# Slab splits and norms of a two-block transformer kernel placed anew, and GpSimd's attention slabs subtracted in eight pieces

## The reference

```python
def ffn_half(h, m, k, g_norm, wi, wo):
    hn = modulate(rmsnorm_2(h, g_norm), m[3 * k], m[3 * k + 1])
    return h + 0.5 * m[3 * k + 2][:, None, :] * swiglu(hn, wi, wo)
...
    hn = modulate(rmsnorm_2(h, norm_g[l, 1]), ml[3], ml[4])      # x * (1 + scale) + shift
    qa, ka, va, qb, kb, vb, uc, gl = project_tokens(hn, w_in[l], qk_g[l], cos, sin)
    ...
    h = h + ml[5][:, None, :] * merge_branches(ya, yb, yc, gl, w_branch[l], w_out[l])
```

## Time and profile before

| what | value |
|---|---|
| median of three runs | 3198.99 us (3192.22 to 3200.24) |
| the profiled execution | 3192.69 us, its span 3190.9 us |
| TensorE busy | 2930.7 us (92%) |
| VectorE, ScalarE, GpSimd busy | 1550.4, 1028.4 and 309.9 us |
| mean granted clock of TensorE | 0.964 |
| the second block | from about 1127 us to the end |

### The profile page before, as it was taken

How to read it: one execution, slowest core, us unless ns; L and a number is a source line. 1 busy time by engine, 2 the same in 40 slices (tenths; PEclk the granted TensorE clock), 3 DMA queues, 4 the chain that set the end, 5 groups by cost and what they waited for, 6 DMA issues and landing times.

```text
span 3190.9 us, 55191 instructions
## 1 busy us (share of the span) xinstructions
PE 2930.7 (92%) x23861; PEld 2389.9 (75%) x23861; DVE 1550.4 (49%) x2194; ACT 1028.4 (32%) x1502; POOL 309.9 (10%) x226
## 2 busy tenths in 40 slices
PE   6998877899999889899899989999899998989899
PEld 6876565677767679877568878888688887769899
DVE  6534244233223356673764434444544457476566
ACT  3211113222222244432642332222422224264543
POOL 5123000000000000122100010000100003210000
PEclk9999888999999989999999999999899999999999
DMA  6346857999889845411012222222122222104552
GB/s 243 132 166 260 328 233 314 419 385 373 353 354 383 353 163 185 146 66 40 1 40 106 106 100 98 92 92 93 66 98 100 92 93 80 53 14 176 200 188 85
DMA packets 77069, 547.83 MB, mean 172 GB/s; under 512 B 8384, under 2 KB 10432, under 8 KB 11056
## 3 DMA queue, kind: packets, MB, share of 16 engines
q1 hardware_dynamic: 76000, 540.05, 43.7%
q0 software_dynamic: 848, 4.53, 0.4%
HBM read 637.87 MB, written 1.05 MB: 200 GB/s over the span
## 4 chain that ended last, share of the span: by engine, by line
PE 79%; DVE 10%; DMA 3%; ACT 3%; issue 3%; POOL 1%; DVEq 0%; POOLq 0%; SPq 0%; ACTq 0%
PE bank L759 56%; PE bank L1117 9%; DMA ring<-slabs 3%; PE bank L1467 2%; DVE clow L2536 1%; ACT whi L1913 1%; PE bank L822 1%; DVE tiny L2691 1%; PE bank L952 1%; PE bank L1555 1%; PE bank L939 1%; DVE wk L2668 1%; PE bank L1536 1%; PE bank L1636 1%; PE bank L1644 1%
## 5 line engine op out<-in xcount | busy, mean ns | idle before, releaser
L759 PE MATMUL bank<-hhi,whi 128*128 128x256 f32 (+1 forms) x1280 | 437.3, 342 | 18.7 <-DVE wlo L2145 18.7
L759 PE MATMUL bank<-hlo,whi 128*128 128x256 f32 (+1 forms) x1280 | 435.8, 340 | 0.0
L759 PE MATMUL bank<-hhi,wlo 128*128 128x256 f32 (+1 forms) x1280 | 432.5, 338 | 0.0
L2145 DVE TENSOR_TENSOR wlo<-ring,whi 128x2048 fp32r<-128x2048 f32 x132 | 298.7, 2288 | 266.0 <-ACT whi L1668 208.1
L759 PE MATMUL bank<-fhl,whi 128*128 128x256 f32 (+1 forms) x1408 | 348.0, 339 | 0.0
L1668 ACT ACTIVATE whi<-ring 128x2048 fp32r<-128x2048 f32 x132 | 251.2, 1908 | 211.1 <-PE bank L759 211.1
L759 PEld LDWEIGHTS bank<-hhi,whi 128*128 128x128 f32 x1280 | 242.6, 190 | 48.4 <-issue 19.8
L1117 PE MATMUL bank<-ring,wk 128*32 128x256 f32 x4064 | 252.8, 392 | 22.0 <-DMA ring<-slabs 13.8
L759 PEld LDWEIGHTS bank<-hhi,wlo 128*128 128x128 f32 x1280 | 245.6, 192 | 29.2
L759 PEld LDWEIGHTS bank<-fhl,whi 128*128 128x128 f32 x1408 | 240.3, 188 | 32.0
L759 PEld LDWEIGHTS bank<-hlo,whi 128*128 128x128 f32 x1280 | 243.0, 190 | 28.1
(11 more groups left out here) (492 smaller groups left out, 5562.6 us busy)
## 6 DMA issues: line engine op xcount, KB each, us to landing
ring<-slabs SPq DMA_DIRECT2D x542, 1024.0 KB
wk<-slabs SPq DMA_DIRECT2D x45, 1024.0 KB, 11.5
ac<-slabs SPq DMA_DIRECT2D x16, 1024.0 KB, 10.5
wk<-mixp POOLq DMA_DIRECT2D x1, 1040.0 KB, 12.5
xt<-xT SPq DMA_DIRECT2D x1, 1024.0 KB, 6.7
xt<-ctxT POOLq DMA_DIRECT2D x1, 1024.0 KB, 6.0
out<-xt SPq DMA_DIRECT2D x4, 256.0 KB, 2.4
cst<-maskc POOLq DMA_DIRECT2D x1, 960.0 KB, 14.7
```

The lines of the kernel that those rows point to most:

```text
L759: last = pe.matmul(o, a, b, start=k == 0, stop=k == len(pairs) - 1)
L2145: tt_(wlo_of(n), slab(n), whi_of(rel).bitcast(F32), ALU.subtract).then_inc(sem("wlo"), 1)
```

## The change

It does five things. (1) In block 0 of an FFN ScalarE splits the gate slab of block 1 before the SiLUs, the up slab of block 1 between the SiLUs and the high halves, and the down slab after those; VectorE splits that up slab before the low halves. (2) In the norms in front of FFNs, VectorE applies the scale together with the root, ScalarE adds the shift as it rounds the high half, and VectorE's subtract adds the shift again; the scales of norm n + 1 are computed at the end of norm n. (3) In norm 4 GpSimd adds only tiles 1 and 2 to tile 0, and TensorE sums six tiles. (4) VectorE's two splits for FFN 3 come before tile 3 of the last but one down product and before tile 2 of the last. (5) GpSimd subtracts an attention slab in eight instructions of 256 columns.

```diff
+def added(n):
+    return 2 + 5 * (n - 4) if n >= 4 else 0
...
             def add_squares(n, T):
-                for j in range(1, 6):
+                for j in range(1, 3 if n == 4 else 6):
...
-                    pool.tensor_tensor(wlo_of(n), slab(n), att_whi(l, i).bitcast(F32), ALU.subtract
-                                       ).then_inc(sem("al"), 1)
+                    for q in range(0, SLAB, FB):
+                        c = slice(q, q + FB)
+                        ins = pool.tensor_tensor(wlo_of(n)[:, c], slab(n)[:, c], att_whi(l, i)[:, c].bitcast(F32),
+                                                 ALU.subtract)
+                    ins.then_inc(sem("al"), 1)
...
             def root_rows(n, T):
-                for j in (0, 6, 7):
+                tiles = (3, 4, 0, 5, 6, 7) if n == 4 else (0, 6, 7)
+                for j in tiles:
...
                 if n >= 3:
                     l, k = (n - 3) // 3, (n - 3) % 3
+                    if ph is not None:
+                        for j in range(KT):
+                            act.wait_ge(sem("hs"), 8 * (n - 3) + j + 1)
+                            for half in range(T // TX):
+                                c = slice(half * TX, (half + 1) * TX)
+                                ins = act.activation(high[j][:, c], HT[:, j, c], ACT.Identity,
+                                                     bias=MOD[:, l, 24 * k + j, half:half + 1])
+                            ins.then_inc(sem("hh"), 1)
+                        return
...
                 def step(b, i):
+                    if b == 0:
+                        split_slab(ph, gate_slab(1))
+                        silu(0, 0, None)
+                        silu(0, 1, None)
+                        split_slab(ph, gate_slab(1) + 1)
+                        high(0, 0, None)
+                        high(0, 1, None)
+                        split_slab(ph, down_slab(ph, 0))
+                        return
...
+            def scales(n):
+                l, k = divmod(n - 3, 3)
+                then(ts_(AMOD, MOD[:, l, 24 * k + 8:24 * k + 16, :], 1.0, None, ALU.add))
+                w = pc("ng", 24 * l + 8 * k, 8).rearrange("p (a b) -> p a b", b=1)
+                then(tt_(AMOD, AMOD, w.to_broadcast([P, 8, 2]), ALU.mult))
...
-                        if j < KT:
+                        if j < KT and ph is None:
                             tt_(HT[:, j, 0:T], XT[:, j, 0:T], root, ALU.mult).then_inc(sem("hs"), 1)
-                        if high is not None and j >= 2:
-                            dve.wait_ge(sem("hh"), h0 + j - 1)
+                        elif j < KT:
+                            for half in range(T // TX):
+                                c = slice(half * TX, (half + 1) * TX)
+                                ins = stt(HT[:, j, c], XT[:, j, c], AMOD[:, j, half:half + 1], root[:, c], ALU.mult,
+                                          ALU.mult)
+                            ins.then_inc(sem("hs"), 1)
...
+                        for half in range(T // TX):
+                            c = slice(half * TX, (half + 1) * TX)
+                            ins = stt(HLO[:, j - 2, c], HT[:, j - 2, c], MOD[:, l, 24 * k + j - 2, half:half + 1],
+                                      high[j - 2][:, c].bitcast(F32), ALU.add, ALU.subtract)
+                        ins.then_inc(sem("hl"), 1)
+                    if n < 8:
+                        scales(n + 1)
...
                 def down(b, i):
                     for m in range(nd):
-                        if after is not None and b == ph["nb"] - 1 and m in (0, 4):
-                            split_slab(after, m // 4)
+                        if after is not None and (b, m) in ((ph["nb"] - 2, 3), (ph["nb"] - 1, 2)):
+                            split_slab(after, b - ph["nb"] + 2)
...
                     product(b, 0, i)
                     product(b, 1, i)
+                    if b == 0:
+                        split_slab(ph, gate_slab(1) + 1)
                     low(b, 0, i)
                     low(b, 1, i)
                     if b or i is not None:
                         down(b - 1, i)
+                    if b and not last:
+                        split_slab(ph, gate_slab(b + 1) + 1, i)
                     if not last:
-                        split_slab(ph, gate_slab(b + 1) + 1, i)
                         split_slab(ph, down_slab(ph, b), i)
```

More of the change, by code:

```diff
@@ L778, in root_rows @@
                     else:
-                        pe.wait_ge(sem("sacc"), count("sacc", 5 * (n - 3)))
+                        pe.wait_ge(sem("sacc"), count("sacc", added(n)))
                     for c in range(rows):
                         mm = pe.matmul(bank[3][0:rows, 0:RCOL], pc("erow", 7 - c, rows), HT[:, j, c * RCOL:(c + 1) * RCOL],
-                                       start=j == c == 0, stop=j == 7 and c == rows - 1)
+                                       start=j == tiles[0] and c == 0, stop=j == 7 and c == rows - 1)
                         if owed[0]:
@@ L2145, in split_slab @@
                 tt_(wlo_of(n), slab(n), whi_of(rel).bitcast(F32), ALU.subtract).then_inc(sem("wlo"), 1)
[L2147 to L2154 removed]
+            def scales(n):
[3 more added lines that the diff above has]
+                then(tt_(AMOD, AMOD, w.to_broadcast([P, 8, 2]), ALU.mult))
+            def norm(n, T, ph=None, h0=None, high=None):
+                l, k = divmod(n - 3, 3)
                 if n == 3:
+                    scales(3)
                     split_slab(ph, 0)
```

14 lines of the change are left out of this document (7 added, 7 removed).

## The result

The changed kernel takes 3148.6 us (median of 4 runs, 3144.7 to 3149.9) against 3199.6 us for the kernel before beside it (3192.2 to 3205.2): ratio 0.984, 95% interval 0.982 to 0.986. Its profiled execution has a span of 3142.9 us at a mean granted clock of 0.969, against 3190.9 at 0.964. The forecast was 3151.

The account below looks back on a forecast made before the run. TensorE, busy 92% of the span, bounds the kernel; gains are its idle or lower-clock time. Terms sum to 44.3 us: 3148.4 from the profiled execution, 3154.7 from the median, middle 3151 us; range 3137 to 3170.

Parts of the forecast that it names:

- Stalls (18.7): Behind the first block of each FFN: four waits for VectorE's low half of a slab go, 18.7 us.
- Clock behind them (7.0): Behind the four first-block stalls: without the idle time TensorE's clock does not fall, 7.0 us (bounds 0 and 8).
- the clock does not come back: Rival, chance 0.20: first-block stalls go but the lower clock stays for some microseconds; 7.8 us missing, 3159 us.
- Fused norm: Norms ahead of the four FFNs: high half ready sooner, 1.3 us each for n=5, 6 and 0.8 for n=3, 8; 4.2 us.
- the low end: Fast end of the range, 3137 us: more gain from clock, first blocks, jobs and cheap pieces, 55 us off 3192.
- Norm 4 (2.9): Norm 4: GpSimd adds two tiles, TensorE sums six in 5.7 us, ending at 1339.6 and not 1342.5; 2.9 us.
- Norm 6 (2.0): Ahead of the third FFN, VectorE's splits move earlier: adds end 1.2 us sooner, half the clock's fall 0.8; 2.0 us.
- Norm 7's scale (1.4): Norm 7: a small VectorE scale instruction, lengthened by GpSimd's subtract, is moved away; 1.4 us.
- the projection (1.6): Projection of layer 1: rotations held less by GpSimd's pieces, 5.3 us, against two later slabs; net 1.6 us.
- The term of the slab: GpSimd's attention slab in eight instructions: 6.2 us against 4.6 in one, 1.6 us more.
- Jobs (6.5): Attention jobs: VectorE's scalings wait at most one GpSimd piece, so TensorE idles less; about 6.5 us.
- The likeliest case: Whole kernel: the forecast itself, all terms gained, 3151 us; chance 0.60.

Follow-up runs that it names:

- the early split alone: Kernel before with only the split of gate slab 1 moved ahead of block 0's SiLUs and products: 3184.7 us, ratio 0.995; repeated, 3185.2 us, 0.996.
- filling the idle time alone: Kernel before, its four stalls kept but filled with repeated TensorE products into an unused bank: 3191.7 us, ratio 0.997.
- the pieces alone: Kernel before with only GpSimd's 22 attention slabs subtracted in eight instructions of 256 columns: 3185.7 us, ratio 0.996.
- the norms alone: Kernel before with only the fused norm ahead of the four FFNs and the scale instructions moved to the norm before: 3192.0 us, ratio 0.998.

## Why the forecast was right, point by point

Us gained, by the first traces of both kernels. The table's stretches count each stall with the clock that it met.

```
                                    forecast   measured
1, 2  splits in block 0, clock        25.7       27.3     first blocks 19.5, clock behind them 7.8
3     fused norm of the FFNs           4.2        6.1     2.0 + 1.6 + 1.6 + 0.9, of it 3.6 clock
4     norm 4                           2.9        3.9     3.0 to the end of the root rows, 0.9 behind
5     norm 6                           2.0        2.7
6, 7  norm 7, projections              3.0        1.5     4.1 - 2.4 - 0.2
7     jobs                             6.5        8.5     2.7 + 5.8
      rest of FFN 3 and 4                        -0.4
sum                                   44.3       49.5     (48.0 in span: norm 3 began 1.5 us later)
```

- **Stalls (18.7).** Right. The idle time before L759 went from 18.7 to 0.6 us, and the early split alone cut the net time by 17.6. The up slab of block 1, with its margin of 0.7 us, is not late.
- **Clock behind them (7.0).** Right in place, size and cause: 15.6 us of lower clock behind the four first blocks, worth 7.8, are none after, and filling the idle time alone gave 9.1. The rival "the clock does not come back" falls in all eight traces with the early split: none has any lower clock there. The forecast gave it 0.20; its argument, that the idle time ahead of each first block remains, was true but it only costs within the first block (8.0 us there after, 12.0 before).
- **Fused norm.** From VectorE's first instruction to TensorE's first matmul of FFN 2 it is 2.0 us now (1861.52 to 1863.48) and was 3.5: 1.5 for the 1.3 that I had. The rest of the surplus is clock, which the shorter idle times met less of; I had left that for the low end.
- **Norm 4 (2.9).** Right to 0.1 us up to the end of the root rows. I had TensorE sum six tiles in 5.7 us, and it took 5.53, and starts the moment it comes free.
- **Norm 6 (2.0).** The adds end 1.2 us sooner, as I had it (a wait of 1.87 for 3.11); of the clock's fall I took half, 0.8, and the whole came back, 1.6 (2.85 for 4.47).
- **Norm 7's scale (1.4) and the projection (1.6).** The term of the scale was right: from the end of the root rows of n=7 to TensorE's next matmul it was 2.44 us and is 0.97. But 0.6 us come back right behind it, where the clock costs 1.0 more than before. The projection term was too large: the projections of layer 1 are 3.2 us shorter, the last slabs take 2.4 back and layer 0 0.2, so 0.6 for 1.6. The scale took 3.96 us because GpSimd's slab held it; with pieces, that cause is gone as well, so moving it adds nothing to the pieces. The sum of the forecast has the gain once, and rightly so. In the kernel with the pieces alone, where the scale stands at its old place, its two instructions take 0.17 and 0.65 us:

```profile
2650.08 0.17 DVE L2155 TENSOR_SCALAR tiny<-mods 128x16 f32<-128x16 f32 x1
2650.29 0.65 DVE L2157 TENSOR_TENSOR tiny<-tiny,par 128x16 f32<-128x16 f32 x1
```

  Norm 7 with its projections is 4.7 us shorter by the pieces alone, 1.0 by the norms alone, and 4.1 by the whole change.
- **Pieces.** The term of the slab was mis-sized: I took 6.2 us, from a duration of 0.733 for each piece, and an undisturbed slab takes 5.55. The durations overlap: pieces start 0.69 us apart and last 0.74, so starts, not durations, are what to multiply. Slabs of 4.61, 5.00, 5.55 and 6.75 us in 1, 4, 8 and 16 instructions give 0.13 to 0.14 us for each further one. The Trainium skill, "GPSIMD Engine Reference", on reconciling measured numbers, has about 156 ns of dispatch for an instruction of VectorE and no figure for GpSimd; the row of GpSimd here is those 0.13 to 0.14 us. Where VectorE comes in between, each time two pieces start 0.18 us later (0.88 apart and not 0.70), which makes the 5.94 and 6.33 us of the chain.
- **What VectorE pays.** The longest scaling is 4.59, 1.50, 0.95 and 0.68 us with pieces of 2048, 512, 256 and 128 columns, that is 0.48 alone and at most about one piece of waiting (the forecast's 0.35 alone is that of the form of 256 columns). That is the forecast's mechanism. In a rotation both instructions on SBUF operands can be held, 0.92 and 0.85 us at most for 0.41 and 0.43 alone: at most 0.9 us together, where I had charged two waits, 1.3 in all. The rule of the Trainium skill, "SBUF — State Buffer", on who interferes with whom (the shared ports are held for one whole instruction, and the other engine fully blocks), agrees with these four sizes.
- **Jobs (6.5).** 8.5, of which 3.4 is clock. I had left the clock in the jobs out of the sum, though each scaling of 4.6 us stops TensorE.
- **The slab on the chain.** I had two slabs of layer 1 late by 1.6 us more; three were on the chain, and the last of them, slab 10, gave back 2.4 us (0.7 net and 1.7 of clock).

The likeliest case was right, and so was its size, but not its make-up, and that the size came out so near is in part luck: the net work was 9.0 us too large and the clock 14.2 too small, and the two cancel for the most part. Clock had 7.8 us of the 44.3, and had 22.0 of the 49.5 between the first traces; net work had 36.5 and had 27.5. As I read the table, both misses have one cause: I priced each idle time at its length, as if TensorE ran at 2.4 GHz around it. Part of the idle time had lain in low stretches, where it costs no work, and each idle time that went took some of a low stretch with it. The median moved by 51 us and the first traces by 48; the first trace of before has the cheaper jobs, and against its second trace the change gives 58.0 us. I had seen that the profiled execution was 6.3 us below the median, and taken the middle. The price of the jobs is a likely reason for such a difference, but how often either price comes is not shown.

## What to carry to other kernels

Split a measured time into span times granted clock, and the rest, before explaining it: the first part repeats within a few us, the second jumps by 14 us between executions of one and the same kernel, and an edit can look half as good as it is. When two edits remove the same stall from two sides, count it once: ask of each what is left of its stall when the other is in. And where one engine's long instruction holds another's, cut it to pieces about as long as the other's typical instruction (here 256 or 512 columns, at 0.13 us for each further piece, with no difference between the two that these runs can tell); pieces of 128 columns cost more net time than they gave.

## What the runs showed of the hardware that I had not expected

- Idle times of 4.7 us behind a first block cost 7.8 us of clock over four places, and 120 matmuls into an unused bank during them win 9.1 back (with standard errors of 1.9 and 1.5 for the two means), with the net time unchanged at 3072.9.
- The same kernel (before), in the attention jobs of layer 0 and just behind them, loses 6.8 or 20.5 us to the lower clock. In one execution of the kernel before, TensorE stays at 1.2 GHz for 17 us there, and in another at 2.4.
- GpSimd's instructions overlap by 0.05 us in a row of pieces: 0.69 us apart with durations of 0.74.
